# Expert routing reordered, and the second stage's expert matrices loaded, awaited and released by halves

## The reference

```python
def grouped_moe(h, router_w, router_bias, w_gate, w_up, w_down):
    scores = jax.nn.sigmoid(t @ router_w)
    sel = scores + router_bias
    ...
    e_idx = top_k(masked, 2)              # masked: the scores of the best of 4 groups
    w = take_along_axis(scores, e_idx); w = w / sum(w)
    for e in range(N_EXPERTS):            # 16 experts, d_ff 512
        he = jax.nn.silu(t @ w_gate[e]) * (t @ w_up[e])
        out = out + gates[:, e:e + 1] * (he @ w_down[e])
```

## Time and profile before

| | us |
|---|---|
| median of 3 runs (1583.53 to 1588.64) | 1585.25 |
| the profiled execution | 1593.78 |
| its span in the profile | 1591.8 |
| TensorE busy with matmuls | 1510.1 (95%) |
| VectorE / ScalarE / GpSimd busy | 603.2 / 420.9 / 62.4 |
| mean DMA rate, 535.77 MB moved | 337 GB/s |
| mean granted clock | 0.973 |

### The profile page before, as it was taken

How to read it: one execution, slowest core, us unless ns; L and a number is a source line. 1 busy time by engine, 2 the same in 40 slices (tenths; PEclk the granted TensorE clock), 3 DMA queues, 4 the chain that set the end, 5 groups by cost and what they waited for, 6 DMA issues and landing times.

```text
span 1591.8 us, 23352 instructions
## 1 busy us (share of the span) xinstructions
PE 1510.1 (95%) x9543; PEld 835.1 (52%) x9543; DVE 603.2 (38%) x1386; ACT 420.9 (26%) x956; POOL 62.4 (4%) x79
## 2 busy tenths in 40 slices
PE   6999989999999999999998999889999999999997
PEld 3665674444446647544443876557544444444433
DVE  3453543233354263533232265443533333233232
ACT  1142332212132333412111353353312121121111
POOL 0000010000010001100000034001000000000000
PEclk9999989999999999999998999899999999999999
DMA  9997799999998777799999300521999999999993
GB/s 353 338 352 280 300 394 405 429 427 427 423 380 315 281 296 323 293 430 427 427 427 410 124 1 1 202 116 48 389 426 426 429 429 428 428 429 428 427 427 167
DMA packets 95717, 535.77 MB, mean 337 GB/s; under 512 B 8047, under 2 KB 11977, under 8 KB 70290
## 3 DMA queue, kind: packets, MB, share of 16 engines
q1 hardware_dynamic: 95218, 534.39, 82.8%
q10 hardware_dynamic: 416, 0.17, 0.0%
HBM read 533.48 MB, written 1.06 MB: 336 GB/s over the span
## 4 chain that ended last, share of the span: by engine, by line
PE 76%; DMA 16%; DVE 3%; ACT 2%; issue 1%; SPq 0%; POOL 0%; POOLq 0%; DVEq 0%; ACTq 0%
PE pair L1112 22%; PE bank L828 6%; PE pair L1135 6%; DMA ring<-in_moe_w_gate_dram 5%; PE bank L1135 5%; DMA hh<-in_w_dram 4%; DMA ring<-in_w_dram 4%; PE bank L1092 4%; PE bank L725 3%; PE pair L1215 3%; PE bank L1148 3%; PE bank L922 2%; PE bank L835 2%; PE pair L804 2%; DMA ring<-in_a_w_qkv_dram 1%; PE bank L1215 1%
## 5 line engine op out<-in xcount | busy, mean ns | idle before, releaser
L1112 PE MATMUL pair<-ring,arena 128*64 128x512 f32 x1664 | 375.2, 604 | 14.1 <-DMA ring<-in_w_dram 7.0
L1112 PEld LDWEIGHTS pair<-ring,arena 128*64 128x64 f32 x1664 | 117.9, 139 | 244.9 <-issue 244.7
L2499 DVE SCALAR_TENSOR_TENSOR xT<-bank,mod,xT 128x256 f32<-128x256 f32 x180 | 75.9, 477 | 173.4 <-PE bank L1148 173.4
L828 PE MATMUL bank<-hh,ring 128*128 128x256 f32 x512 | 117.3, 386 | 2.2 <-DMA ring<-in_a_w_qkv_dram 2.2
L828 PEld LDWEIGHTS bank<-hh,ring 128*128 128x128 f32 x512 | 96.8, 192 | 24.4 <-issue 8.7
L2485 DVE SCALAR_TENSOR_TENSOR arena<-sq,arena,pair 128x512 f32<-128x512 f32 x32 | 35.6, 1111 | 175.4 <-PE pair L1112 175.4
L1135 PE MATMUL pair<-ring,arena 128*64 128x512 f32 x416 | 96.7, 607 | 1.4 <-DMA ring<-in_w_dram 0.7
L1135 PE MATMUL bank<-ring,arena 128*64 128x512 f32 x416 | 93.7, 592 | 0.0
L1112 PE MATMUL pair<-arena 128*64 128x512 f32 x192 | 86.3, 603 | 4.7 <-DMA hh<-in_w_dram 4.7
L1838 ACT ACTIVATE arena<-pair 128x512 f32<-128x512 f32 x32 | 19.1, 597 | 266.7 <-PE pair L1173 266.7
L1112 PE MATMUL pair<-hh,arena 128*64 128x512 f32 x192 | 86.3, 603 | 0.0
(11 more groups left out here) (438 smaller groups left out, 2143.6 us busy)
## 6 DMA issues: line engine op xcount, KB each, us to landing
ring<-in_w_dram SPq DMA_DIRECT2D x70, 2048.0 KB, 25.1
ring<-in_moe_w_down_dram SPq DMA_DIRECT2D x28, 2048.0 KB, 16.6
ring<-in_moe_w_gate_dram SPq DMA_DIRECT2D x26, 2048.0 KB, 16.8
ring<-in_moe_w_up_dram SPq DMA_DIRECT2D x26, 2048.0 KB, 18.8
ring<-in_ada_w_dram SPq DMA_DIRECT2D x24, 2048.0 KB, 17.6
ring<-in_w_mod_dram SPq DMA_DIRECT2D x12, 2048.0 KB, 12.1
arena<-in_w_dram SPq DMA_DIRECT2D x12, 2048.0 KB, 24.2
hh<-in_w_dram SPq DMA_DIRECT2D x12, 2048.0 KB, 28.6
```

What stands on the lines that cost most here:

```text
L828: last = mm(b[i % 2][:, 0:S], w[:, k, cols(s4)], hh[:, k, 0:S], start=(k == 0), stop=(k == KT - 1))
L1112: last = mm(b[2 + m][half(a), :], x_sel[:, k, half(a)], expert_slot(l, a, c, m)[:, k, :], start=(k == 0), stop=(k == KT - 1))
L2499: last = stt(xT[:, k, :], (sums_last if last_pair else sums)[r][:, k % 2 * S:(k % 2 + 1) * S], mod[:, l, G2 + k:G2 + k + 1], xT[:, k, :], ...
```

## The change

Routing, all layers: `affine_by_row` is split: blocks 0 to 5 are computed before the wait for the mask, 6 and 7 behind the rank product. The count of tokens per expert goes behind the gather, into bank 7. The first projection and `spread_out(0)` go ahead of TensorE's wait for `n_ready` and its read of the loop count. VectorE computes the pick and the affine rows first, then the gates, then the slots; the round count follows the first gathered tokens. `gate_act` moves from `sq` to the first half of `y_sel`, with a wait for `y_rest` before SiLU.

Layer 1: the context's transposes go behind the first projection (banks 0, 4, 5, 7), its copies and squares behind the first SiLU; its sum of squares goes ahead of the last pair (bank 5), and its norm on ScalarE and VectorE to the last pair. Every gate, up and down pair is loaded in halves of the contraction, each with its own semaphore (6 in place of 3), awaited by the half, and released by the half; `down` runs its contraction in two halves, both output halves in each.

```diff
-        gate_act = sq[:, 0:FF]
         y_sel = view(4096, D)
+        gate_act = y_sel[:, 0:FF]
...
+        context_banks = (b[0], b[4], b[5], b[7])
...
-            MOE[l]["full"] = [sem(f"experts_full{q}_{l}") for q in range(3 if l == 1 else 4)]
+            MOE[l]["full"] = [sem(f"experts_full{q}_{l}") for q in range(6 if l == 1 else 4)]
...
-            def both(l, m, i, c, parts=1):
+            def both(l, m, i, c, parts=1, waits=None):
...
-                    if parts == 2:
-                        sp.wait_ge(MOE[l]["gate_ps"], h + 1)
+                    if parts == 2 and waits:
+                        sp.wait_ge(*waits[h])
...
+                if l == 1:
+                    if not last or c < 3:
+                        both(l, 0, i + 1, c + 1, 2, ((gate, 2 * i + 1), (gate, 2 * i + 2)))
+                        both(l, 1, i + 1, c + 1, 2, ((up, 2 * i + 1), (up, 2 * i + 2)))
+                        both(l, 2, i + 1, c + 1, 2, ((down, 3 * i + 1), (down, 3 * i + 3)))
+                    return
...
-                if l == 1:
-                    pe.wait_ge(table_in, 64)
-                    pe.wait_ge(score_ready, 2)
-                    turn_tokens(lambda t, k: ctx_tok[:, t, cols(k)], turned, 4)
-
-                if l == 1:
-                    pe.wait_ge(act_step, 4)
+                affine_by_row(l, range(6))
                 pe.wait_ge(mask_ready, turn(mask_ready))
                 mask = route_mask(l)
                 mm(b[7][:, 0:2 * E], K(C_TRI), mask[:, :, :], start=True, stop=False)
                 mm(b[7][:, E:2 * E], ones, mask[:, 0, :], start=False, stop=True).then_inc(rank_ps, 1)
-                affine_by_row(l)
-                for t in range(TT):
-                    last = mm(b[4][:, 0:E], ones, mask[:, t, :], start=(t == 0), stop=(t == TT - 1))
-                last.then_inc(rank_ps, 1)
+                affine_by_row(l, range(6, KT)).then_inc(rank_ps, 1)
...
                     for k in range(KT):
+                        if k % 4 == 0:
+                            arrived(j, c, m, first, k // 4)
...
-                        if k == KT - 1 or (first and k == 3):
+                        if k == KT - 1 or (k == 3 and (first or l == 1)):
                             last.then_inc(M["up_ps" if m else "gate_ps"], 1)
...
+                    for h in range(parts):
+                        arrived(j, c, 2, False, h)
+                        for n in range(2):
+                            for f in range(h * wide, (h + 1) * wide):
...
+                            if h + n >= 1 or parts == 1:
+                                last.then_inc(M["down_ps"], 1)
...
                 gather_first(0)
                 gather_first(1)
+                E = EXPERTS[l]
+                for t in range(TT):
+                    last = mm(b[7][:, 2 * E:3 * E], ones, route_mask(l)[:, t, :], start=(t == 0), stop=(t == TT - 1))
+                last.then_inc(rank_ps, 1)
+                project(0, 0, 0, True)
+                spread_out(0)
                 pe.wait_ge(n_ready, l + 1)
                 if l == 1:
-                    summed_squares(28)
+                    pe.wait_ge(table_in, 64)
+                    pe.wait_ge(score_ready, 2)
+                    pe.wait_ge(col_ready, AFFINE_ROWS[l])
+                    turn_tokens(lambda t, k: ctx_tok[:, t, cols(k)], turned, context_banks)
                 m = pe.value_load(nit[0:1, 2:3], min_val=1, max_val=ROUNDS * EXPERTS[l] // 8 - 1)
-                project(0, 0, 0, True)
-                spread_out(0)
...
+                    if l == 1 and c == 0:
+                        pe.wait_ge(act_step, 4)
...
+                    if l == 1 and last_pair:
+                        pe.wait_ge(rt_ready, 5)
                     down(j, c)
...
+                    if l == 1 and c == 3:
+                        summed_squares(28, b[5])
                     pair_of(m, c, c == 3)
...
                     if not last_pair:
+                        act.wait_ge(M["y_rest"], 4 * i + 4)
                         gate_out(i + 1)
...
                 gate_out(0)
+                if l == 1:
+                    context_squares()
+                act.wait_ge(n_ready, l + 1)
+                m = act.value_load(nit[0:1, 0:1], min_val=1, max_val=ROUNDS * EXPERTS[l] // 2 - 1)
                 with act.Fori(0, m) as i:
                     pair_of(i, False)
+                if l == 1:
+                    context_norm()
                 pair_of(m, True)
...
                 with dve.Fori(0, m) as i:
                     pair_of(i, False)
+                if l == 1:
+                    norm(cT, gainc)
                 pair_of(m, True)
```

More of the change, by code:

```diff
@@ L481, in following @@
                 gate, up, down = MOE[l]["done"]
+                if l == 1:
[4 more added lines that the diff above has]
+                    return
                 if not last or c < 3:
-                    if not first:
+                    if first:
+                        both(l, 1, i + 1, c + 1, 2, ((gate, 1), (gate, 2)))
+                    else:
                         sp.wait_ge(gate, i + 2)
-                    both(l, 0 if l == 1 else 1, i + 1, c + 1, 2 if first else 1)
+                        both(l, 1, i + 1, c + 1)
                     sp.wait_ge(up, i + 1)
-                    both(l, 1 if l == 1 else 2, i + 1, c + 1)
-                if not last or c < (3 if l == 1 else 2):
+                    both(l, 2, i + 1, c + 1)
+                if not last or c < 2:
                     sp.wait_ge(down, 2 * i + 2)
-                    if l == 1:
-                        both(l, 2, i + 1, c + 1)
-                    else:
-                        both(l, 0, i + 2, c + 2)
+                    both(l, 0, i + 2, c + 2)
             def further(l, r, j, c):
@@ L500, in further @@
                 if l == 1:
[L501 to L506 removed]
+                    both(l, 0, i, c, 2, ((gate, 2 * at - 1), (gate, 2 * at)))
+                    both(l, 1, i, c, 2, ((up, 2 * at - 1), (up, 2 * at)))
+                    both(l, 2, i, c, 2, ((down, 3 * at - 2), (down, 3 * at)))
                 else:
@@ L557, in after_experts @@
                     last = k // 2 if l == 1 else (2, 0, 1)[k // 2]
-                    steps = (1, 1, 2)[last]
-                    behind = (1, 0, 0 if l == 1 else -2)[last]
+                    steps = ((2, 2, 3) if l == 1 else (1, 1, 2))[last]
+                    behind = 0 if l == 1 else (1, 0, -2)[last]
                     sp.wait_ge(MOE[l]["done"][last], more_rounds[l] * (N * steps) + (N * steps + behind))
@@ L757, in router_row, with affine_by_row @@
                 last.then_inc(row_ps, 1)
-            def affine_by_row(l):
+            def affine_by_row(l, ks):
                 pe.wait_ge(col_ready, EIGHT_READY[l])
-                for k in range(KT):
-                    mm(affine_ps[:, k * 16:(k + 1) * 16], eight_ids[:, k::KT], affine[:, l, :], start=True, stop=True)
+                for k in ks:
+                    last = mm(affine_ps[:, k * 16:(k + 1) * 16], eight_ids[:, k::KT], affine[:, l, :], start=True, stop=True)
+                return last
             def logits(l, k):
@@ L1094, in gather, with arrived @@
                     last.then_inc(M["gathered"], 1)
-                def arrived(j, c, m, first=False):
+                def arrived(j, c, m, first=False, h=0):
                     q = place(l, c, m)
-                    turns = 4 * j + c if l == 1 else 3 * j + (3 * c + m) // 4
-                    pe.wait_ge(M["full"][q], 32 * turns + (64 if q == 0 and not first else 32))
+                    if l == 1:
+                        pe.wait_ge(M["full"][2 * q + h], 32 * (4 * j + c) + 32)
+                    elif h == 0:
+                        turns = 3 * j + (3 * c + m) // 4
+                        pe.wait_ge(M["full"][q], 32 * turns + (64 if q == 0 and not first else 32))
                 def project(j, c, m, first=False):
                     i = 4 * j + c
-                    arrived(j, c, m, first)
                     if m == 0:
@@ L1197, in experts, with turn_tokens @@
                 pe.wait_ge(M["added"], m * 16 + 18)
-            def turn_tokens(src, last_sem, first=1):
+            def turn_tokens(src, last_sem, banks=b[1:5]):
                 for k in range(KT):
                     for t in range(TT):
-                        last = nc.tensor.transpose(b[first + k // 2][:, cols(k % 2 * TT + t)], src(t, k), ident)
+                        last = nc.tensor.transpose(banks[k // 2][:, cols(k % 2 * TT + t)], src(t, k), ident)
                     if k % 2 == 1:
@@ L2391, in route @@
                     choose(l, r["sel"])
-                    mask = route_mask(l)
-                    gate = r["gate"]
-                    then(tt(gate, mask, score, ALU.mult))
-                    then(nc.vector.tensor_reduce(r["total"], gate, AX.X, ALU.add))
-                    then(nc.vector.reciprocal(r["inv"], r["total"]))
```

(16 more changed lines are left out.)

76 lines of the change are left out of this document (27 added, 49 removed).

## The result

Over 20 runs each the changed kernel takes 1576.23 us (1570.2 to 1584.34) and the kernel before 1585.97 (1581.26 to 1588.74): ratio 0.9943, 95% interval 0.9932 to 0.9954, 9 to 10 us faster where 17 were forecast. Its profiled execution took 1573.54 us, span 1571.6.

The account below looks back on a forecast made before the run. TensorE was taken to bound the first stage, the DMA stream the second and third; gains of 3.5, 10.6 and 2.85 us sum to 17.0, taking the median 1585.25 to 1568.3 us, range 1557 to 1579.

Parts of the forecast that it names:

- rival (b): Second-stage gate projections: two short waits each may leave TensorE at 1.2 GHz; 4.9 us lost, 1573 us; chance 20%.
- 3.0 and 0.5 for the clock: First routing: 12 affine matmuls hidden in TensorE's idle time gain 3.0 us, a faster clock 0.5.
- 4.3 and 0.5: Second routing: first projection starts 4.3 us earlier through moved affine and context work, plus 0.5 us for the clock.
- 2.35 and 0.5: Third routing: 2.35 of 2.97 us of affine matmuls hidden in idle time, plus 0.5 us for the clock.
- The clock's thermometer: Second routing: affine matmuls' unchanged 3.97 us read as short gaps not keeping the fast clock; 0.5 us taken a stage.
- case (c): Routings and second stage's tail: with gaps filled the clock stays up, 11.9 us more gain, 1556 us; chance 12%.
- g comes 4.8 + 1.9 = 6.7 us earlier: Second stage: last gate matrices land 6.7 us earlier, 4.8 from the stream's earlier start, 1.9 from closed gaps.
- I take 428: Second-stage stream: halves with 8 KB runs keep 428 GB/s, taken from a row from 656 to 661 at 431.
- Rival (a): Second-stage stream: halves lower the rate, to 387 GB/s costing 21.8 us, 1590 us; chance 5%.
- 3.5 + 2.3 - 1.9 = 3.9: Second stage's end, last pair: 3.5 us from the shorter last gate half, 2.3 from the clock, less 1.9 of costs.
- The clock term: Second stage's last pair: shorter waits recover half of 4.6 us of slow clock, 2.3 us.
- Costs set at nothing: Second stage mainly: context transposes (2.7 us without cover), SyncE's doubled issues, the `y_rest` wait and loop count cost nothing.

Follow-up runs that it names:

- after_third: The changed kernel with no edit, profiled a third time: 1576.08 us, ratio 0.9935 to the kernel before; its profiled span was 1582.6 us.
- before_again: The kernel before with no edit, profiled a second time: 1585.64 us, ratio 1.0007; span 1583.9 us.
- after: The changed kernel's first profiled execution: 1573.54 us, span 1571.6; median over 20 runs 1576.23 us, ratio 0.9943.
- after_again: The changed kernel with no edit, profiled a second time: 1575.0 us, ratio 0.9939; span 1574.2 us.
- whole: The changed kernel with the second stage's matrices loaded, awaited and released whole as before: 1577.96 us, ratio 0.9959.
- halves_only: The kernel before with only the second stage's halves added, routing and context as before: 1581.63 us, ratio 0.9981.
- route02: The kernel before with the second stage's halves and the reordered routing in the first and third stage only: 1576.79 us, ratio 0.9936.
- runs_8k: The kernel before with each second-stage matrix loaded by two DMAs split by contraction, released and awaited whole: 1590.47 us, ratio 1.0021.
- merged: The changed kernel with one DMA for the same half of a pair's two matrices, 8 KB runs kept: 1575.56 us, ratio 0.9942.

## Why the prediction was right, and where it was off

**Direction and mechanism were right, the size nearly double.** 17.0 were forecast; 9.5 are accounted for between like executions, and 9.7 are the medians' difference. The time lies inside the range, but its upper part was there for rival (b), which did not come: that the range held is in part luck.

**Routings.** First: forecast 3.0 and 0.5 for the clock; measured 3.0 and nothing. Second: 4.3 and 0.5; measured 4.14. In after_third they were 1.6 and 5.4, near the same sum. Third: 2.35 and 0.5; measured 3.0 with TensorE at full clock (2.8 of affine matmuls, 0.1 of the gather and 0.4 because the count of tokens takes 0.46 us behind the gather and took 0.86 ahead of it, less 0.25 by which the rank product comes later), and a routing no shorter than before's where it was at half. The forecast left that condition out.

**The clock's thermometer was broken.** The forecast took the affine matmuls' 3.97 us as a sign that TensorE stood at 1.2 GHz in the second routing too. They tell nothing: 12 of them take 2.85 us at a granted clock of 0.50 and 2.92 at 1.00 (rows above), and in the profiled kernel before the 3.94 us of the first routing were at 0.50, the 3.97 of the second at 0.91. The transposes do tell: 1.92 us for eight at the one, 1.04 at the other. In before_again's first routing the second eight already took 1.92 us, ahead of the idle time and the rank product; in the profiled kernel before they took 1.04, and the clock fell later. In the change, where no gap follows, the same eight took 1.88 and 1.92 (after, after_again). So the clock falls there with the gap filled as well, and case (c) did not come in the first routing.

**The second stage: "g comes 4.8 + 1.9 = 6.7 us earlier" failed.** Measured from the start of routing 2, the last gate matrices land at 19.23 + 196.89 = 216.1 us in before_again (843.63, the start that the wait ends in) and at 15.09 + 198.96 = 214.1 in after_again: 2.1 earlier. Of the 6.7, 4.14 came from the start; 3.1 went to the rate (79.7 MB ahead of that landing, at 421 rather than 428); the rest, some 1.0, is what the gaps gave, of the 1.9 forecast. The failed step is "I take 428", from a row of 5 us at 431. In that row four halves were alone in flight, and it is too short: cut into stretches of 5 us, the time from 690 to 820 us reads 419 to 442 GB/s in the kernel before and 416 to 426 in after. Five microseconds are no measurement of 1.6%. Rival (a) was right in kind, at a sixth of its price: its bound came from 2 KB runs. The forecast's sign, 428 throughout, failed, and 421 is just above the 420 that it names as wrong.

**The stage's end was right.** Forecast from g on: 3.5 + 2.3 - 1.9 = 3.9. Measured 32.43 us from landing to decay product in before_again, 28.58 in after_again: 3.85. In it the last half projection takes 3.65 where the whole took 8.57, 3.44 of size and 1.48 of clock, and 1.07 are costs, 0.70 of them the context's sum of squares. The clock term was too large because its rows came from an execution with 4.6 us of slow clock there; in before_again it was 1.5, and in after_third 1.7 of it is back, in the first `down` half. Those 3.1 us, and 3.7 more in its third stage (465.60 to 461.89), make up most of the 8.5 us by which the profiled execution stood above the median. Subtracting 17 from the median assumed that a typical run has them to lose.

**Rival (b) did not come.** The gate halves behind waits of 0.94, 1.33 and 1.43 us took 3.65, the full clock's time. The Trainium skill's "TensorE: Matmul & The Clock Gate", section "HAM oscillation", has bursts between DMA waits start cold. At waits this short no gate half here agrees; behind 2.66 us (8.57) the trace does. The wait's length alone does not decide it: the same projection behind nearly the same wait in before_again, and then in `whole`:

```profile
784.18 8.78 PE L1112 MATMUL pair<-ring,arena 128*64 128x512 f32 x32 [1.93 <-DMA ring<-in_moe_w_gate_dram]
...
775.70 7.09 PE L1118 MATMUL pair<-ring,arena 128*64 128x512 f32 x32 [1.91 <-DMA ring<-in_moe_w_gate_dram]
```

What else decides it stays open.

**Costs set at nothing.** The context's transposes were said to cost nothing, under cover of the stream. They cost the stream itself: they delay the first up projection and with it the release that the stream waits for (399 to 400 GB/s over 18 us where `halves_only` has 422). The last gate matrices land 1.16 us later than in `halves_only` (198.96 to 197.80 from the first projection); with the 0.70 this is the 1.9 us between the two kernels. `y_rest`, SyncE's issues and the loop count cost nothing that a row shows, as forecast.

**Between the decay product and routing 3** the forecast had no term. 2.0 us of the shortfall are there.

In sum, with terms read from the same two traces: 17.0, less 3.1 for the rate, 0.9 for gaps, 0.7 for the second routing and its clock, 0.5 and 0.5 for the clocks of the other two, 2.0 behind the decay product and 0.3 in the third stage itself, plus 0.65 for the third routing, is 9.65; the segments gave 9.5.

## What to carry to other kernels

When a stream of DMAs sets the end, cutting its pieces buys an earlier start and an earlier last piece, and pays in rate on every byte: compare the two over the whole stream, and take the rate from tens of microseconds of pieces of that form. Read a term that rests on the clock from two executions at least, and read the clock from rows whose time follows it. Work that is moved into a gap is hidden only as long as the engine reaches the gap in time: in the third routing here 2.1 us of delay ahead of it were enough to put most of it in the way.

## What the hardware showed that was not expected

DMAs of 1 MiB to 64 partitions, two for each matrix and many in flight, carried 220 GB/s where 128 partitions carried 427, with the same 16 KB packets: a packet took 1600 / (1678 - 334) = 1.19 us instead of 0.61. The cause was not tested further. The Trainium skill's "DMA: Bandwidth & Descriptors", section "The descriptor swizzle", says that partitions 0 to 63 are written through the even and 64 to 127 through the odd of 16 ports; a DMA to one half would then use eight, and 220 to 427 agrees with that.

Halving the contiguous run from 16 to 8 KB costs 1.6% of a full stream (428 to 421 GB/s), in five kernels alike (after, `halves_only`, `route02`, `runs_8k`, `merged`), and halving the number of DMAs at 8 KB gives none of it back.

Small float32 matmuls with a 128x128 weight load (128x16 outputs) take the same at both clock levels, 0.24 us each.
